# Token-shifted projection evictions and earlier small steps in two projection stages of a four-layer hybrid model

## The reference, cut to what matters

```
p = p + (token_shift(p) - p) * mu
r, k, v, wd, ad, gd = split(p)
w_log = -softplus(-(w0 + tanh(wd) @ w_up)) - 0.5;  decay = exp(-exp(w_log))
a = sigmoid(a0 + ad @ a_up);  g = sigmoid(gd) @ g_up
kk = k * k_k;  kk = kk * rsqrt(max(sum(kk * kk), 1e-24))
k_mod = k * (1 + (a - 1) * k_a);  y = rwkv7_scan(r, decay, k_mod, v, -kk, kk * a)
```

## Time and profile before

| | us |
|---|---|
| median of 3 runs | 3190.88 (3189.2 to 3192.65) |
| profiled execution, its own time | 3197.68 |
| its span, first to last instruction | 3195.8 |
| PE busy | 2847.8 |
| DVE busy | 1923.4 |
| ACT busy | 1363.9 |

### The profile page before, as it was taken

The page is one execution under the profiler, slowest core; times in us unless marked ns, Lnnn a source line. Parts: engine busy times, 40 slices in busy tenths (PEclk is TensorE's granted clock), DMA queues, the critical chain, the costliest instruction groups (busy, mean ns, idle before and its releaser), DMA issues. The chain is left out here.

```text
span 3195.8 us, 54124 instructions
## 1 busy us (share of the span) xinstructions
PE 2847.8 (89%) x23292; PEld 2444.9 (77%) x23292; DVE 1923.4 (60%) x2596; ACT 1363.9 (43%) x1882; POOL 151.9 (5%) x116
## 2 busy tenths in 40 slices
PE   7898678999897778999998998889999989988899
PEld 6787557888786657888886875678988878757788
DVE  5754766966655766956565444666565654446564
ACT  5413334655313344645453232545454632325443
POOL 0030000000130000000000210000000012000000
PEclk9998889999997889999998998999999988989999
DMA  5211114564111123555542111245555411203453
GB/s 216 93 41 53 66 53 145 201 216 160 65 54 53 66 92 133 201 185 185 199 146 75 40 67 40 94 146 204 207 193 192 146 62 40 80 27 121 144 199 131
DMA packets 54669, 386.21 MB, mean 121 GB/s; under 512 B 6688, under 2 KB 7328, under 8 KB 8352
## 3 DMA queue, kind: packets, MB, share of 16 engines
q1 hardware_dynamic: 54432, 382.76, 34.4%
HBM read 381.69 MB, written 1.05 MB: 120 GB/s over the span
## 5 line engine op out<-in xcount | busy, mean ns | idle before, releaser
L321 PE MATMUL banks<-normed_high,weights_high 128*128 128x256 f16 (+1 forms) x4096 | 1138.9, 278 | 36.8 <-DVE weights_low L307 20.1
L322 PE MATMUL banks<-normed_low,weights_high 128*128 128x256 f16 (+1 forms) x4096 | 1137.7, 278 | 0.0
L323 PE MATMUL banks<-normed_high,weights_low 128*128 128x256 f16 (+1 forms) x4096 | 1136.8, 278 | 0.0
L307 DVE SCALAR_TENSOR_TENSOR weights_low<-weight_ring,weights_high 128x2048 f16<-128x2048 f32 x334 | 761.2, 2279 | 400.9 <-ACT weights_high L301 386.4
L301 ACT ACTIVATE weights_high<-weight_ring 128x2048 f16<-128x2048 f32 x306 | 580.0, 1898 | 271.8 <-PE banks L323 259.7
L321 PE MATMUL banks<-projected,weights_high 128*128 128x256 f16 x1696 | 470.6, 277 | 72.8 <-DVE projected L332 72.8
L321 PEld LDWEIGHTS banks<-normed_high,weights_high 128*128 128x128 f16 (+1 forms) x4096 | 408.2, 100 | 114.0 <-issue 29.8
L322 PE MATMUL banks<-projected,weights_high 128*128 128x256 f16 x1696 | 470.8, 278 | 0.0
L323 PE MATMUL banks<-projected,weights_low 128*128 128x256 f16 x1696 | 470.5, 277 | 0.0
L323 PEld LDWEIGHTS banks<-normed_high,weights_low 128*128 128x128 f16 (+1 forms) x4096 | 407.6, 100 | 55.2
L322 PEld LDWEIGHTS banks<-normed_low,weights_high 128*128 128x128 f16 (+1 forms) x4096 | 407.4, 99 | 54.4 <-issue 1.3
(11 more groups left out here) (391 smaller groups left out, 3291.5 us busy)
## 6 DMA issues: line engine op xcount, KB each, us to landing
weight_ring<-w SPq DMA_DIRECT2D x356, 1024.0 KB, 4.9
small_weights<-small SPq DMA_DIRECT2D x2, 1280.0 KB, 7.3
constants<-const SPq DMA_DIRECT2D x1, 1601.0 KB, 10.2
weight_ring<-w SPq DMA_DIRECT2D x2, 640.0 KB, 3.9
residual<-xt SPq DMA_DIRECT2D x1, 1024.0 KB, 5.1
small_weights<-small SPq DMA_DIRECT2D x2, 512.0 KB, 10.4
out<-residual SPq DMA_DIRECT2D x4, 256.0 KB, 2.9
parameters<-par SPq DMA_DIRECT2D x2, 115.5 KB, 9.6
```

The costliest lines, as they stand in the source:

```text
L307: nc.vector.scalar_tensor_tensor(out=self.part(self.mem.w_low, g), in0=self.part(self.mem.ring, g), scalar=W_SCALE, in1=self.part(self.mem ...
L321: pe.matmul(out, w_high, high, start=start, stop=False, skip_group_check=skip)
L322: pe.matmul(out, w_high, low, start=False, stop=False, skip_group_check=skip)
L323: return pe.matmul(out, w_low, high, start=False, stop=stop, skip_group_check=skip)
```

## The change

In the rwkv stages each of tiles 0 to 13 is now copied from PSUM twice: unscaled by anything but `PART_X` into a new buffer `raw`, and by a column `keep = PART_X * (1 - mu)` into `projected`. The shift is then one instruction for a tile, `p[:, 1:] += raw[:, :-1] * mu`, two tiles after each low half from 3 to 9. The key chain moves up: squares at 7, sum at 6, guard at 9, root at 7, inverse at 10, spread at 11. Gates, exps and the steps that feed the bonus move up by one or two; `bonus_values` and `operands_near` move from the end to 15 and 16, and the two copies of `operands_far` go to ACT at 15 (`operands_copied`). In the delta stages the columns and values are turned at 11, the spreads of q and k run after group 12 instead of after group 13, two copies go from DVE to ACT, k is turned into bank 3, the root moves from 12 to 11. In every project stage the high halves of the next stage's first two jobs are made inside the loop, as soon as their slot is free, where before they followed the last group.

```diff
+            if i == 0 and beside.keep is not None:
+                need("mu_kept", 1)
             for n, (g, c0, m, part, tile) in enumerate(grp):
-                ins = nc.scalar.activation(mem.proj[part:part + m, tile, :],
-                                           mem.ps[part:part + m, i % BANKS, n * T:(n + 1) * T],
-                                           ACT.Copy, scale=PART_X)
+                got, scale = mem.ps[part:part + m, i % BANKS, n * T:(n + 1) * T], PART_X
+                if beside.keep is not None and tile < 14:
+                    nc.scalar.activation(beside.raw[:, tile, :], got, ACT.Copy, scale=PART_X)
+                    scale = beside.keep[:, tile:tile + 1]
+                ins = nc.scalar.activation(mem.proj[part:part + m, tile, :], got, ACT.Copy,
+                                           scale=scale)
             ins.then_inc(sig("bank_free"), 1)
-            while split_up_to < jobs[-1] and used[split_up_to + 1 - RING] <= i + 1:
+            while (split_up_to < jobs[-1] + ahead and
+                   used[split_up_to + 1 - RING] <= i + 1):
                 split_up_to += 1
                 stream.high(act, nc, sig, split_up_to)
...
-        for g in range(jobs[-1] + 1, jobs[-1] + 1 + ahead):
-            stream.high(act, nc, sig, g)
...
-        self.vector = {9: [self.shift_low_rank], 10: [self.shift], 11: [self.keys_squared],
-                       12: [self.decays_summed], 13: [self.decays_centred],
-                       14: [self.keys_guarded, self.keys_mixed],
-                       15: [self.keys_inverse, self.bonus_products], 16: [self.keys_unit],
-                       "end": [self.bonus_values, self.operands_near, self.operands_far,
-                               self.operands_state]}
-        self.scalar = {7: [self.low_rank_in], 9: [self.gates_of_a], 12: [self.exps],
-                       13: [self.keys_root], "end": []}
-        self.tensor = {8: [self.low_rank_up], 10: [self.keys_sum], 14: [self.keys_spread],
-                       15: [self.bonus_sum], "end": []}
+        self.keep = cut(14)
+        self.raw = cut.buffer[:, 18 * T:32 * T].rearrange("p (a t) -> p a t", a=14)
+        self.vector = {"begin": [self.mu_kept],
+                       3: [self.shift(0)], 4: [self.shift(2)], 5: [self.shift(4)],
+                       6: [self.shift(6)], 7: [self.shift(8), self.keys_squared],
+                       8: [self.shift(10)], 9: [self.keys_guarded, self.shift(12)],
+                       10: [self.keys_inverse], 11: [self.decays_summed],
+                       12: [self.decays_centred], 13: [self.keys_mixed, self.bonus_products],
+                       14: [self.keys_unit], 15: [self.bonus_values], 16: [self.operands_near],
+                       "end": [self.operands_far, self.operands_state]}
+        self.scalar = {7: [self.keys_root, self.low_rank_in], 8: [self.gates_of_a],
+                       11: [self.exps], 15: [self.operands_copied], "end": []}
+        self.tensor = {6: [self.keys_sum], 8: [self.low_rank_up], 11: [self.keys_spread],
+                       13: [self.bonus_sum], "end": []}
...
+    def shift(self, first):
+        def step(link, say, need):
+            need("bank_free", first // 2 + 1)
+            for i in (first, first + 1):
+                p = self.mem.proj[:, i, 1:T]
+                say(self.nc.vector.scalar_tensor_tensor(out=p, in0=self.raw[:, i, 0:T - 1],
+                                                        scalar=self.col("mu", i), in1=p,
+                                                        op0=ALU.mult, op1=ALU.add), "shifted")
+        return step
...
         self.vector = {4: [self.gate_sizes], 7: [self.gate_sums],
-                       "end": [self.units_inverse, self.unit_q, self.unit_k, self.columns,
-                               self.operands, self.by_token]}
-        self.scalar = {3: [self.gate_logs], 8: [self.gate_exp], "end": []}
-        self.tensor = {5: [self.beta_spread], 11: [self.units_sum],
-                       "end": [self.spread_q, self.spread_k, self.gate_spread, self.turn_v,
-                               self.turn_k]}
+                       "end": [self.columns, self.values_by_token, self.units_inverse, self.unit_q,
+                               self.unit_k, self.operands, self.operands_gated]}
+        self.scalar = {3: [self.gate_logs], 8: [self.gate_exp],
+                       "end": [self.queries_copied, self.keys_copied]}
+        self.tensor = {5: [self.beta_spread],
+                       11: [self.units_sum, self.turn_columns, self.turn_v],
+                       12: [self.spread_q, self.spread_k],
+                       "end": [self.turn_k, self.gate_spread]}
...
-        self.scalar[12] = [self.units_root]
+        self.scalar.setdefault(11, []).append(self.units_root)
```

More of the change, by code:

```diff
@@ L492, in vector @@
         loaded(dve)
+        for step in beside.vector.get("begin", ()):
+            step(link, say, need)
         for n, g in enumerate(jobs[2:]):
@@ L1236, in q64, with mu_kept @@
         return flat(ap).rearrange("p (q t) -> p q t", t=HD)
[L1240 to L1253, removed]
+    def mu_kept(self, link, say, need):
+        mu = self.mem.par[:, C1["mu"]:C1["mu"] + 14]
+        say(self.nc.vector.tensor_scalar(self.keep, mu, -PART_X, PART_X, ALU.mult, ALU.add), "mu_kept")
+    def shift(self, first):
[7 more added lines that the diff above has]
+        return step
     def keys_squared(self, link, say, need):
@@ L1327, in operands_near, with halves, operands_copied @@
                              q64(self.p_r), q64(z[7]), ALU.mult))
-        link(V.tensor_tensor(flat(self.bt), flat(z[1]), flat(z[5]), ALU.mult))
-        link(V.tensor_tensor(flat(self.kt), flat(self.p_k), flat(z[5]), ALU.mult))
+        say(V.tensor_tensor(flat(self.bt), flat(z[1]), flat(z[5]), ALU.mult), "near_ready")
+        say(V.tensor_tensor(flat(self.kt), flat(self.p_k), flat(z[5]), ALU.mult), "near_ready")
+    def halves(self):
+        return [[v.rearrange("p a (b q t) -> p (a b) q t", b=2, q=2) for v in pair]
+                for pair in ((self.bt, self.btp), (self.kt, self.ktp))]
+    def operands_copied(self, link, say, need):
+        for i, (n4, f4) in enumerate(self.halves()):
+            need("near_ready", i + 1)
+            link(self.nc.scalar.copy(f4[:, :, 1, :], n4[:, :, 1, :]))
     def operands_far(self, link, say, need):
         V = self.nc.vector
-        for near, far in ((self.bt, self.btp), (self.kt, self.ktp)):
-            n4, f4 = (v.rearrange("p a (b q t) -> p (a b) q t", b=2, q=2) for v in (near, far))
-            link(V.tensor_copy(f4[:, :, 1, :], n4[:, :, 1, :]))
+        for n4, f4 in self.halves():
             link(V.tensor_tensor(f4[:, :, 0, :], n4[:, :, 0, :],
@@ L1412, in keys_spread @@
     def keys_spread(self, pe, need):
+        need("decay_sigmoid", 4)
         need("kk_inverse", 1)
@@ L2495, in operands, with values_by_token @@
         link(V.tensor_tensor(self.qh, self.q[:, :, b1], spread, ALU.mult))
-    def by_token(self, link, say, need):
+    def values_by_token(self, link, say, need):
         V = self.nc.vector
@@ L2539, in spread_q @@
     def spread_q(self, pe, need):
+        need("columns", 1)
         need("unit_inverses", 1)
@@ L2556, in gate_spread, with turn_columns @@
     def gate_spread(self, pe, need):
-        ps, mem = self.mem.ps, self.mem
-        need("gate_exp", 1)
         need("unit", 1)
         for i in range(MT_):
-            pe.matmul(ps[:, 2, i * P:(i + 1) * P],
-                      mem.c("hsel", MT_ * P)[0:HEADS, i * P:(i + 1) * P], self.egsum[:, P:T],
-                      start=True, stop=True)
+            mm = pe.matmul(self.mem.ps[:, 2, i * P:(i + 1) * P],
+                           self.mem.c("hsel", MT_ * P)[0:HEADS, i * P:(i + 1) * P],
+                           self.egsum[:, P:T], start=True, stop=True)
+        mm.then_inc(self.sig("gate_spread"), 1)
+    def turn_columns(self, pe, need):
+        need("gate_exp", 1)
+        need("beta", 1)
         for w, src in enumerate((self.gsum, self.beta)):
@@ L2582, in turn_k @@
         need("unit", 2)
-        need("beta_keys", 1)
         for i in range(MT_):
-            mm = pe.transpose(self.mem.ps[:, 6, i * P:(i + 1) * P], self.k[:, i, 0:P],
+            mm = pe.transpose(self.mem.ps[:, 3, i * P:(i + 1) * P], self.k[:, i, 0:P],
                               self.mem.c("ident"))
@@ L2856, in first_block @@
     angles = Angles(nc, mem, p_sig)
-    rwkv.vector[3] = [angles.of_positions, angles.sine_angle]
-    rwkv.vector[5] = [angles.cosine_angle]
+    rwkv.vector[3] += [angles.of_positions, angles.sine_angle]
+    rwkv.vector[5] += [angles.cosine_angle]
     rwkv.scalar[4] = [angles.sines]
```

31 lines of the change are left out of this document (18 added, 13 removed).

## The result

Five runs of the changed kernel have a median of 3163.4 us (3161.3 to 3175.0); five of the kernel before, on the same chip, 3190.9 (3189.2 to 3194.9). The ratio is 0.9923, with a 95% interval of 0.9901 to 0.9945: faster by 0.8%, clear of 1. The five runs lie in two groups, three at 3161.3 to 3163.4 and two at 3172.9 and 3175.0. The profiled execution took 3162.5 us for a span of 3160.4.

What follows compares the result with a forecast made beforehand. The prediction took PE as the bound, busy 2848 of 3196 us, so gains come from its waits or slow clock. Terms of 10.7, 12.0 and 2 x 2.6 made 27.9 us: 3163 against 3190.9, with 3156.5 to 3170.5 holding 8 in 10.

Steps and rivals of the forecast that it cites:

- The loop's cover: Rwkv loop: four copies take 1.4 us, ACT works 3.3 of a 5.24 us group, so the added copies cost nothing.
- `keys_squared` in time: Rwkv loop, tightest place: done at 769.0, against 770.1 when group 6 ends and `keys_sum` wants it; holds by 1.1 us.
- Low rank: Ahead of `low_rank_up`: PE waits 1.0 instead of 1.62 us, gain 0.6; in the first rwkv stage 2.3, loss 0.7.
- Key chain: At `keys_spread` in rwkv: the 3.15 us wait goes; matmuls take 1.86 instead of 3.36 us, gain 1.5 at 2.4 GHz.
- The tail: End of the second rwkv stage: last eviction ends it, next stage at 836.1 instead of 847.06, gain 10.9 us.
- The next stage's transposes: Behind the rwkv barrier: 16 transposes take 2.2 instead of 3.3 us at the faster clock, gain 1.1.
- Delta: End of the delta stages: PE pauses 2.9 us where it paused 5.5, gain 2.6 each.
- Sum: All four stages: 10.7 + 12.0 + 2 x 2.6 = 27.9 us gained.
- The clock: Rival: spreads and transposes stay at 1.2 GHz, a slow stretch follows the first stage's wait; gain 21, 3170 us; chance 17%.
- the rival that the clock gives more: Delta's small matmuls start at 2.4 GHz, saving up to 2.5 us each: 3158 us; chance 8%.
- None of the others: Rivals: a new wait at the end, 3171 us, 5%; gain lost to weight waits in the next stages, 3190, 3%.
- the slower one: Rival: ACT becomes the bound through double evictions; break-even at 1.33 us a copy, 3201 us at 1.5; chance 4%.

Runs made afterwards that it cites:

- e7: The changed kernel with four more raw copies of each of tiles 0 to 13, work of no use: 3176.1 us, before on that chip 3198.2.
- e10: The changed kernel with two more raw copies of each of tiles 0 to 13, work of no use: 3164.4 us, before on that chip 3201.8.
- e5: The changed kernel with the key chain late again (exps 12, root 13, spread 14, inverse 15, unit 16): 3166.4 us, before on that chip 3198.2.
- e8: The changed kernel with twelve matmuls of no use ahead of the barrier in all four stages: 3164.9 us, before on that chip 3198.2.
- e9: The changed kernel run again without any edit, on another chip: 3163.6 us, before on that chip 3201.8.
- e2: The kernel before with only the next stage's high halves made early, in the loop: 3196.9 us, before on that chip 3196.8.
- e4: The kernel before with the changed kernel's delta steps and early high halves: 3191.1 us, before on that chip 3196.8.
- e12: The kernel of e6 with twelve matmuls of no use ahead of the barrier in the delta stages alone: 3159.0 us, before on that chip 3201.8.
- e11: The same kernel as e6, run again on the chip of e9: 3157.6 us, the changed kernel there 3163.6.
- e6: The changed kernel with guard at 8, root at 6 and tanh's table loaded there too: 3157.9 us, before on that chip 3198.2.

## Why the prediction was right, step by step

- **The loop's cover.** Predicted: four copies in 1.4 us, ACT 3.3 us of 5.24. Measured 1.26 and 3.2. The copy with a pointer for its scale takes 0.47 to 0.49 us beside 0.38 (predicted: 0.5), and e7 and e10 put the end of the loop's cover between two and four more copies a tile.
- **`keys_squared` in time.** Predicted with 1.1 us to spare: it ends at 760.27, and `keys_sum` starts at 761.22 behind group 6, 0.95 us later. e10 shows that this is the first thing to give way.
- **Low rank.** Predicted waits 1.0 and 2.3 us; measured 0.87 and 2.29. On the Trainium skill's rule that a table switch costs a drain beyond its load (ScalarE: Activation LUTs, What ACT_TABLE_LOAD costs), the trace of after disagrees again: load from 770.94 to 772.22, activation at 772.24.
- **Key chain.** No wait of PE at L1141, and 1.97 us for 32 (1.9 from start to start) where 1.86 was predicted. e5 adds what the prediction had not separated: moving the chain wins 3.0 us at PE's wait and 4.3 at the barriers, and pays 1.6 of it back ahead of `low_rank_up`.
- **The tail.** From the start of the stage the prediction put PE's last matmul at 101.4 us, DVE's end at 98.8, ACT's copies at 100.1 and the next stage at 103.7. Measured, from 723.7: 101.3, 98.4, 99.7 and 103.4. The last eviction ends the stage, as predicted; pause 2.17 (predicted 2.3), and 1.68 in the first stage. Up to the barrier the lead grows by 11.2 us (predicted 10.9), in the first stage by 10.0 (predicted 9.6).
- **The next stage's transposes.** Predicted 2.2 us. In the first stage 16 take 1.94 at 2.4 GHz and PE then waits 0.41 for a low half; in the second the clock falls half-way and they take 2.6. This term failed in the second stage. There the slow stretch shrank from 6.8 us to 3.4 and moved: it lasts from 828.2 to 831.7, over the last transposes and the fill tile. The transposes win 1.0 us and the fill tile loses it, so the lead behind the barrier grows by nothing where 1.1 was predicted; in the first stage it grows by 1.3.
- **Delta.** Predicted pause 2.9 us and gain 2.6 each. Pauses 2.98 and 2.94, and the lead at the barriers grows by 2.7 and 2.6. What comes on top is clock: 0.3 in the first stage, at the end of its slow stretch, and 0.3 in the second, whose first small matmuls run at 2.4 GHz (0.1 of it goes again).
- **Sum.** 27.9 predicted, 28.4 measured over the four stages: 11.3, 11.3, 3.0 and 2.8, where 10.7, 12.0, 2.6 and 2.6 were predicted. The sum came closer than its terms, because the second rwkv stage was 0.7 us worse and the others 1.2 better.
- **The rivals.** The clock was the one that mattered: the slow stretch behind the first stage's 2.29 us wait does appear, in e8, e9 and e10, and cost 3.3 us in e9 (the rival had 1.7). Of the rest of that rival, one transpose term of 1.1 us came, in the second stage; the spreads and the first stage's transposes ran at 2.4 GHz. Of the rival that the clock gives more, 0.3 us came behind one delta barrier. None of the others came. e7 shows the slower one to be real but far: with about 3 us more work of ACT in a group, a group loses 1.2 us. e10 shows that 1.6 us more already costs a wait of 0.59 us a stage.
- **The baseline.** The median came out within 0.4 us of the forecast, and that much is luck: it is the highest of the three runs in the lower group, and with one more run among the upper ones it would have been some 10 us higher. What the argument fixes is 28 us over four stages. Elsewhere the kernel before had 3196.8, 3198.2 and 3201.8, and the same edit was worth 38 us on the chip of e9, without a step of the argument being different.

## What to carry to other kernels

A barrier waits for the last of several engines, so write down when each arrives, from the start of the stage: moving the high halves won 12.7 us here and nothing while DVE was last. Extra work on an engine is free up to its idle time per group and then costs in full; the two lengths (3.2 of 5.24 us) say it before a run does. Look also for the step with the least time to spare behind that engine: here it had 0.95 us where the loop had 2.05. When two profiles of a kernel whose clock moves are compared, align them by matmul and keep the stages that the edit touches apart from the rest.

## What the runs showed of the hardware that was not expected

- **Levels of one kernel.** e10 gave 3163.5, 3164.1, 3164.7 and 3172.9 us. Its profiled execution was the slowest; against e9's, one piece of the last mixer explains 6.9 us of it. e9, then e10:
```profile
2757.30:2875.06 117.76, 100.03 (x603) 70.81 (x600) 59.21 (x117) 39.28 (x92) 0.00 (x0) 0.90 0.15 54
```
```profile
2757.70:2882.39 124.69, 106.67 (x603) 74.31 (x601) 59.22 (x117) 39.34 (x92) 0.00 (x0) 0.85 0.15 51
```
  It is the same pair of lengths as in before and after. Over the fourteen profiles this piece takes 124 to 125 us in six (before, e2, e4, e8, e10, e12) and 116 to 118 in the other eight. All three kernels with the rwkv stages of before are among the six. That the edit does not set the length is likely, since e10's other runs are 8 to 9 us faster with the same program, but no kernel was profiled at both lengths. What sets it was not tried; e12 arrives there 5 us earlier than e11 and takes 124 us where e11 takes 118.
- **A busy PE can be slow.** The small matmuls of the delta stage fall to 1.2 GHz after 3.1 us without a pause and then run at 0.50 for 10.2 us in which PE is busy throughout (e12). Whether their form brings this or the pause of 1.52 us ahead of them is not shown. Without the added matmuls the changed kernel has 17.1 us at 0.50 there, with PE busy for 16.4 (1705.50).
- **A table can be loaded ahead** by an activation of 128x1 that takes 0.20 us beyond the load's 1.28 (e6).
